# Modulation matmuls in four column groups of the array, summed by the small transposes

## The reference, cut to what matters

```python
def _modulation(cond, w, b):
    m = jax.nn.silu(cond) @ w + b
    return jnp.split(m[:, None, :], 6, axis=-1)

def _modulate(x, shift, scale):
    return x * (1 + scale) + shift

def second_block(x, c, ctx, c_ctx, ada_w, ada_b, ...):
    for i in range(DEPTH):
        ml = _modulation(c, ada_w[i], ada_b[i])
        mc = _modulation(c_ctx[None, :], ada_w[i], ada_b[i])
        hl = _modulate(x, ml[0], ml[1])
        ...
```

## Time and profile before

| | |
|---|---|
| median of 3 runs | 2637.54 us |
| span of the profiled execution (first to last instruction) | 2634.1 us |
| around the span | about 3.4 us to the median |
| PE busy | 2453.1 us, 93% |
| PE weight loads busy (they overlap PE) | 1958.3 us, 74% |
| DVE busy | 1378.3 us, 52% |
| ACT busy | 1260.6 us, 48% |
| line 763 on PE | 768 records, 176.6 us |
| mean granted PE clock | 0.977 |

### The profile page before, as it was taken

The page is one execution under the profiler, slowest core; times in us unless marked ns, Lnnn a source line. Parts: engine busy times, 40 slices in busy tenths (PEclk is TensorE's granted clock), DMA queues, the critical chain, the costliest instruction groups (busy, mean ns, idle before and its releaser), DMA issues.

```text
span 2634.1 us, 33862 instructions
## 1 busy us (share of the span) xinstructions
PE 2453.1 (93%) x13500; PEld 1958.3 (74%) x13500; DVE 1378.3 (52%) x2376; ACT 1260.6 (48%) x2162; POOL 0.2 (0%) x4
## 2 busy tenths in 40 slices
PE   6999899999989999899999999898999997798997
PEld 6844799985469997578767667585777885658987
DVE  3433565553346556554555555436666436346664
ACT  5453554455355546544434434324655423535663
POOL 0000000000000000000000000000000000000000
PEclk9999999999999999999999999999999999899998
DMA  6654254465524442222212112121222221303442
GB/s 241 220 181 155 97 183 170 160 224 199 195 70 170 169 174 80 80 80 96 96 64 80 48 64 80 43 100 49 96 96 86 93 100 59 111 3 142 161 164 91
DMA packets 45433, 314.38 MB, mean 119 GB/s; under 512 B 4791, under 2 KB 6967, under 8 KB 8036
## 3 DMA queue, kind: packets, MB, share of 16 engines
q1 hardware_dynamic: 45284, 312.28, 33.6%
HBM read 311.19 MB, written 1.07 MB: 119 GB/s over the span
## 4 chain that ended last, share of the span: by engine, by line
PE 82%; DVE 8%; ACT 7%; issue 3%; DMA 0%; SPq 0%; ACTq 0%; DVEq 0%
PE bank L651 53%; PE bank L656 8%; PE bank L763 7%; DVE ws L1371 2%; ACT ws L1000 2%; PE bank L672 2%; PE bank L893 2%; DVE xs L1387 1%; PE bank L708 1%; PE bank L803 1%; PE bank L863 1%; PE bank L875 1%; PE bank L906 1%; PE bank L784 1%; PE bank L748 1%
## 5 line engine op out<-in xcount | busy, mean ns | idle before, releaser
L651 PE MATMUL bank<-xs,ws 128*128 128x256 f32 (+1 forms) x9936 | 1636.9, 327 | 106.9 <-issue 52.1
L651 PEld LDWEIGHTS bank<-xs,ws 128*128 128x128 f32 x9936 | 1461.9, 194 | 286.3 <-issue 69.4
L1371 DVE TENSOR_TENSOR ws<-ring,ws 128x1024 fp32r<-128x1024 f32 x468 | 552.4, 1222 | 309.0 <-ACT ws L1000 308.4
L1000 ACT ACTIVATE ws<-ring 128x1024 fp32r<-128x1024 f32 x468 | 468.5, 1049 | 296.0 <-PE bank L651 283.5
L1387 DVE TENSOR_TENSOR xs<-arena,xs 128x512 fp32r<-128x512 f32 (+1 forms) x286 | 161.9, 581 | 315.1 <-ACT xs L1016 314.3
L1016 ACT ACTIVATE xs<-hT 128x256 fp32r<-128x256 f32 (+1 forms) x344 | 171.5, 513 | 288.4 <-PE bank L651 210.7
L1016 ACT ACTIVATE xs<-arena 128x512 fp32r<-128x512 f32 (+1 forms) x286 | 148.9, 539 | 332.5 <-PE bank L651 219.9
L1387 DVE TENSOR_TENSOR xs<-hT,xs 128x256 fp32r<-128x256 f32 (+1 forms) x344 | 183.8, 545 | 182.5 <-ACT xs L1016 180.9
L656 PE MATMUL bank<-ws,xs 128*128 128x512 f32 (+1 forms) x1008 | 229.2, 388 | 14.5 <-DVE ws L1371 10.4
L656 PEld LDWEIGHTS bank<-ws,xs 128*128 128x128 f32 x1008 | 188.4, 189 | 54.8 <-DVE ws L1371 12.0
L763 PE MATMUL bank<-arena,cs 128*2 128x256 f32 x768 | 176.6, 384 | 0.1
(11 more groups left out here) (217 smaller groups left out, 1484.8 us busy)
## 6 DMA issues: line engine op xcount, KB each, us to landing
ring<-in_stream SPq DMA_DIRECT2D x235, 1024.0 KB, 4.8
arena<-in_side SPq DMA_DIRECT2D x56, 1024.0 KB, 4.9
arena<-in_tokens SPq DMA_DIRECT2D x1, 2048.0 KB, 10.9
arena<-bias_vectors SPq DMA_DIRECT2D x1, 1536.0 KB, 7.9
out<-arena SPq DMA_DIRECT2D x1, 1024.0 KB, 4.1
arena<-in_params SPq DMA_DIRECT2D x1, 918.0 KB, 6.4
arena<-bias_vectors SPq DMA_DIRECT2D x1, 706.0 KB, 9.5
con<-in_consts SPq DMA_DIRECT2D x1, 447.5 KB, 3.2
```

Source lines behind the costliest of these rows:

```text
L651: ins = mm(ps(n, 0, g.T), a[wi][:, p * P:(p + 1) * P], x[xi], start=first, stop=last)
L1000: do(ws[:, i % 2, 0, c], ring[:, w % R, c], ACT.Copy).then_inc(w_high, 1)
L1371: ins = v.tensor_tensor(ws[:, i % 2, 1, c], ring[:, w % R, c], ws[:, i % 2, 0, c].bitcast(F32), ALU.subtract)
```

## The change

The stationary operand of the modulation grows from 2 to 32 columns, of which 2 hold the conditions and 30 are zero (`cs` is cleared once at the start by DVE, and ACT waits for that in `small_ready`). The eight chunks of the contraction go in turn to four column groups of the array: chunk k writes partitions 32 (k mod 4) to 32 (k mod 4) + 31 of the bank. The first round of four starts the sums, the second ends them. ACT then copies all 128 partitions of the row piece. The two transposes become two fp32 matmuls with that copy as the stationary operand (128 x 128) and a new constant, `strips` (128 x 2), as the moving one; it has a 1 in each of rows 32 g + j, column j, so the product transposes and adds the four groups.

```diff
--- before.py
+++ after.py
@@ -143,6 +143,7 @@
     p.add("rope", 256)
     p.add("tri", 256)
     p.add("pick", 127)
+    p.add("strips", 2)
     return p
 
 
@@ -402,7 +403,7 @@
         qk = region(o("qk"), (16, T))
         x2 = region(o("x2"), (2, T))
         x3 = region(o("x3"), (2, 16, 16))
-        arow = region(o("x3"), (2, T))[0:2]
+        arow = region(o("x3"), (2, T))
         vn = region(o("vn"), (3, 2, T))
         vsw = region(o("vsw"), (2, 140))
         mixed = region(o("mixed"), (KD, T))
@@ -435,7 +436,7 @@
 
 
         mod = sb("mod", [P, DEPTH, 96])
-        cs = sb("cs", [P, 16])
+        cs = sb("cs", [P, KD, 32])
         scrap = sb("scrap", [P, DEPTH])
         o = Plan()
         for name, n in (("xm", MK * T2), ("xc", MK * T2), ("v", MK * T2), ("qk", 4 * T2), ("P", 6 * T2),
@@ -760,13 +761,14 @@
                             pe.wait_ge(bank_free[n % BANKS], n // BANKS)
                         if i < ADA_W:
                             for k in range(KD):
-                                ins = mm(bank[n % BANKS][0:2, 0:T], cs[:, 2 * k:2 * k + 2], wd[:, k, :],
-                                         start=(k == 0), stop=(k == KD - 1))
+                                c = 32 * (k % 4)
+                                ins = mm(bank[n % BANKS][c:c + 32, 0:T], cs[:, k, :], wd[:, k, :],
+                                         start=(k < 4), stop=(k >= 4))
                         if i:
                             pe.wait_ge(mod_rows, seen(mod_rows))
                             for g in range(2):
-                                ins = nc.tensor.transpose(ps(n, T + 2 * g, T + 2 * g + 2),
-                                                          arow[:, (i - 1) % 2, g * P:(g + 1) * P], ident[0:2, 0:2])
+                                ins = mm(ps(n, T + 2 * g, T + 2 * g + 2), arow[:, (i - 1) % 2, g * P:(g + 1) * P],
+                                         con_at("strips", 2), start=True, stop=True)
                         ins.then_inc(bank_full[n % BANKS], 1)
                     if 0 <= i - 2 < NU:
                         j = i - 2
@@ -981,7 +983,7 @@
             seen = Count()
             own = Count()
             do = nc.scalar.activation
-            act_.wait_ge(small_ready, 2)
+            act_.wait_ge(small_ready, 3)
             act_.wait_ge(dma_par, 32)
 
             fed = {"w": 0, "q": 0}
@@ -1045,7 +1047,7 @@
                 act_.wait_ge(bank_full[N("xT", k) % BANKS], N("xT", k) // BANKS + 1)
                 do(xT[:, k, :], ps(N("xT", k)), ACT.Copy).then_inc(bank_free[N("xT", k) % BANKS], 1)
             act_.wait_ge(bank_free[N("xT", KD - 1) % BANKS], N("xT", KD - 1) // BANKS + 1)
-            do(cs[:, :], par_at("cond", 0, 16), ACT.Silu).then_inc(cs_ready, 1)
+            do(cs[:, :, 0:2], par_at("cond", 0, 16).rearrange("p (a b) -> p a b", a=KD), ACT.Silu).then_inc(cs_ready, 1)
             for l in range(DEPTH):
                 norm_squares(("down", l - 1) if l else None)
                 rstd(N(("rms1", l)), T, D)
@@ -1110,7 +1112,7 @@
                     if i < ADA_W:
                         n = N(("ada", l, i))
                         act_.wait_ge(bank_full[n % BANKS], n // BANKS + 1)
-                        do(arow[:, i % 2, :], bank[n % BANKS][0:2, 0:T], ACT.Copy).then_inc(mod_rows, 1)
+                        do(arow[:, i % 2, :], ps(n, 0, T), ACT.Copy).then_inc(mod_rows, 1)
                     if 0 <= i - 1 < NU and UNITS[i - 1]["kind"] == "sb":
                         s = sbuf[:, (i - 1) % 3, :]
                         act_.wait_ge(arg_ready, seen(arg_ready))
@@ -1406,6 +1408,7 @@
 
             v.memset(eps[:, :], EPS).then_inc(small_ready, 1)
             v.memset(one[:, :], 1.0).then_inc(small_ready, 1)
+            v.memset(cs[:, :, :], 0.0).then_inc(small_ready, 1)
             v.memset(cbias, NEG).then_inc(dve_own, 1)
             dve.wait_ge(dve_own, own(dve_own))
             dve.wait_ge(dma_par, 32)
@@ -1881,6 +1884,7 @@
     pick = np.zeros((P, 127))
     pick[:, 63] = 1
     put("pick", pick)
+    put("strips", np.tile(np.eye(32, 2), (4, 1)))
 
     t = np.arange(T)
     inv = np.float32(10000.0) ** (-np.arange(16, dtype=np.float32) / np.float32(16))
```

## The result

The changed kernel is slower: 2685.89 us against 2637.99 us, a ratio of 1.0173 (95% interval 1.0159 to 1.0188). The forecast was 2590 us with a range of 2553 to 2624; rival B, 2652 us, had the sign but not the cause.

A forecast was written before the change was run, and what follows sets the result against it. TensorE (PE) was taken as the bound. Per layer, 19 x (-1.51 + 0.33) = -22.4, -1.5 and +0.2 give -23.7 us; two layers -47.4, so 2590 us against 2637.5, range 2553 to 2624.

The forecast's parts named there:

- rival B: Modulation matmuls: column groups do not overlap in fp32, so each step is 0.33 us longer; 2652 us, slower; chance 0.16.
- What is late next: Full attention step: falls to 4.69 us; the DVE/ACT loop of 2.8 us and side weights stay shorter, so PE remains the bound.
- the last seven: End of each layer's attention loop: step 24 has the sum and no modulation matmuls, costing +0.2 us.
- ScalarE's chain covers it: Step 0 of the attention: its low clock, 0.72 over 6 us, was taken as hidden behind ACT's chain.
- "sb" steps: Steps 1 to 4, ACT also full: PE's saving mostly becomes waits of 1 to 2 us; -1.5 us for steps 0 to 4.
- Four groups: Modulation matmuls: each of eight matmuls adds one pass instead of two; transposes come at 2.03 us, saving 1.51 us a step.
- Rival A: Modulation matmuls: groups independent pass by pass, 1.2 us in place of 3.54; 2558 us in all; chance 0.18.
- the hand-out of 0.06 us: Modulation passes: can't be handed out faster than line 731's rows, one every 0.06 us, giving a 1.2 us floor.
- The sum: After the modulation: two transposes become two fp32 matmuls of two passes each, +0.33 us a step, range 0.25 to 0.4.
- Weight loads: Modulation matmuls: loads grow from 2 to 32 columns, under 0.216 us, hidden if they may run beside a neighbour's pass.
- rival D: Modulation matmuls: loads can't run beside another column group's matmul; +3.9 +0.33 us a step, about 2797 us; chance 0.03.
- the forecast's own 2578 to 2608: Whole kernel: range from 0 to 0.06 us exposed a matmul and 0.25 to 0.4 for the sum; chance 0.5.

## Why the prediction was wrong

*The step that failed* is in "What is late next": "With the step at 5.87 - 1.51 + 0.33 = 4.69 us". It took every other duration of the step, 2.12 us of them, from a trace at full clock and left them as they were. A full step was forecast to be 1.18 us shorter than before and is 0.73 longer; the 19 full steps of a layer were to save 22.4 us and cost 10.9, and the last seven, forecast at +0.2, cost 7.9.

I had seen that step 0 runs at 0.72 and set it aside since ScalarE's chain covers it. But what the change takes away is what brought the clock back there. The runs show the chain. The clock falls in step 0's logits, before and after the change. Before, it is back within step 0; in the change it stays at half (0.50 over 5.80 us without a gap). Four-group steps don't win it back later either (steps 4 to 23, and the steps around 12 and 13). Where one-group steps or fillers win it back and none of the long waits follows, the change gains (one group up to step 4 or 7, a filler in every step, fillers in steps 0 to 4).

The waits of the "sb" steps are a second obstacle, and not the first. I had forecast waits of 1 to 2 us there without asking what they do to the clock. Before, the 16 passes in a row in every step filled them: 21.60 us busy of 21.60. The run with fillers in step 0 shows that a wait of 2.80 us takes a clock that is full.

The Trainium skill, "TensorE: Matmul & The Clock Gate", Part 1, tells to avoid idle gaps of TensorE between bursts and says that a busy engine gets the full clock. The first fits in kind: the clock fell within the wait of 2.80 us. The second does not fit by the time line: 125.30 us busy of 125.30 at 0.50.

*Four groups*: 2.03 us forecast from the start of the modulation to the sum, 1.00 measured at full clock (163.66 to 164.66), 1.87 at half. My choice rested on the two passes of one matmul keeping the next chunk back. They don't: the loads and passes go out in rounds of four groups. Rival A was right in kind, and even its floor of 1.2 us was too high, since the hand-out of 0.06 us a pass that I took from line 731 is no bound: the 16 passes span 1.07 us, and with 0.38 for the last they start every 0.046 on average.

*The sum*: +0.33 forecast, +0.26 measured. *Weight loads*: hidden, as forecast, and beside passes in other groups too; rival D is refuted. *Rival B*: no overlap; refuted by the 92.8 us. What B would cost is what the one-group run took, 2655 against 2652.

*The "sb" steps*: -1.5 us forecast to step 5's logits. They come 28.4 us after the first logits (132.31 to 160.69), before it was 27.5: +0.9, at half clock.

*What would have been*: with A's overlap and the clock kept, 19 x (5.87 - 3.57) = 43.7 us a layer; the run with four groups from step 5 saves 42.1 in a layer's attention (150.8 to 108.7).

*The range*: the forecast's own 2578 to 2608 does not follow from the terms it names. A saving of 1.51 less 0.25 us a step gives about 2587, one of 1.03 less 0.4 about 2611. The measured time is far outside either.

*Open*: the stretch behind the attention, which the change does not touch, is 3 to 11 us longer in the profiles of all nine changed kernels than in the one profile of the kernel before (1877.0 us there, 1880.1 to 1888.1 in them). It goes with the clock granted in that stretch: 0.98 in the two shortest (before, and fillers in steps 0 to 4), 0.97 in the eight others. One kernel alone varies like this too: the kernel before ran between 2634.64 us at a mean clock of 0.977 and 2644.43 at 0.971. So it is not shown that these microseconds come from the change. What sets how often the clock falls there, and why the first logits come anywhere from 127.3 to 133.1 us, I have not tested.

Nor do the runs say what in a step brings the clock back. In the change it came back near the end of the last seven steps, some 19 us after they began, in both layers. These steps hold no modulation matmuls. With a filler beside the four-group passes it took some 20 us. So steps without four-group passes bring it back about as slowly as steps with them and a filler, and leaving such passes out is not the only way; which property of a step does it was not varied.

## What to carry to other kernels

Before taking matmul time out of a stretch, look at what that time was filling: if TensorE waits for another engine there, the saved time becomes a wait, and the clock can go with it. Look also at where the clock falls and what brings it back, since the change may remove just that. Check the granted clock of the same stretch before and after, not the busy share. Where packed matmuls save time, leave the dense form in the steps that are bound by another engine, where it costs next to nothing: with one group in steps 0 to 4, step 5's logits came 28.6 us after the first, in the change 28.4.

## What the hardware showed that I had not expected

- Four column groups of fp32 passes (128 x 32 stationary, 256 moving) overlap almost wholly: 16 passes in 1.07 us against 3.64 in one group at full clock. At half clock four groups take 1.93; the 6.15 us of one group are from a step in which the clock came back before its end.
- The same sequence of instructions ran at 1.00 in one kernel and at 0.50 in another, for 100 us and more each, with TensorE busy without a gap in the latter. What decided was the clock it met, as steps 11 to 15 show within one kernel.
- Filler matmuls that nobody reads made the change 4 to 5% faster, one in every step or two in each of steps 0 to 4. Four in step 0 alone did nothing for it (2681.74 us).
